# Differential attention weights: two diagonal products on TensorE per block, or one combination on VectorE and a transpose

## What is computed

```
s = jnp.einsum('bqhcd,bkhcd->bchqk', qi, kf) * scale
s = jnp.where(mask, s, NEG_INF)
p = jax.nn.softmax(s, axis=-1)
w = p[:, 0] - lam * p[:, 1]
return jnp.einsum('bhqk,bkhd->bqhd', w, vf)
```

## Time and profile before, and how to read it

| | |
|---|---|
| median of 3 runs | 3783.66 us (3781.82 to 3785.66) |
| the profiled execution | 3782.0 us |
| its span | 3780.2 us |
| PE, PEld, DVE, ACT, POOL busy | 3536.2, 3345.4, 2086.2, 1083.3, 1947.7 us |
| mean granted TensorE clock | 0.97 |
| stage_m in the span | about 469 to 869 us |

### The profile page before, as it was taken

The page is one execution under the profiler, slowest core; times in us unless marked ns, Lnnn a source line. Parts: engine busy times, 40 slices in busy tenths (PEclk is TensorE's granted clock), DMA queues, the critical chain, the costliest instruction groups (busy, mean ns, idle before and its releaser), DMA issues. The chain is left out here.

```text
span 3780.2 us, 57577 instructions
## 1 busy us (share of the span) xinstructions
PE 3536.2 (94%) x22880; PEld 3345.4 (88%) x22880; DVE 2086.2 (55%) x3740; ACT 1083.3 (29%) x1181; POOL 1947.7 (52%) x735
## 2 busy tenths in 40 slices
PE   8999967888897999999999999997999999999997
PEld 8988743547897999999999999997999999999997
DVE  4212076426102899975444544453677777777773
ACT  3111032334212232333333333332222222222222
POOL 3333207004334445665655666654676676666762
PEclk9999978898998999999999999998999999999999
DMA  5577676562321224777777777777778878777872
GB/s 215 199 289 297 235 181 222 173 216 103 140 107 71 85 91 163 261 284 277 277 277 285 280 276 276 286 270 284 285 282 305 296 282 301 295 286 293 301 290 95
DMA packets 254404, 891.46 MB, mean 236 GB/s; under 512 B 99057, under 2 KB 132338, under 8 KB 177266
## 3 DMA queue, kind: packets, MB, share of 16 engines
q1 hardware_dynamic: 179026, 548.32, 41.3%
q0 software_dynamic: 36864, 268.45, 17.3%
q10 hardware_dynamic: 38368, 72.83, 5.5%
HBM read 818.45 MB, written 68.71 MB: 235 GB/s over the span
## 5 line engine op out<-in xcount | busy, mean ns | idle before, releaser
L111 POOL TENSOR_TENSOR wl<-raw,wh 128x2048 fp32r<-128x2048 f32 x324 | 1524.5, 4705 | 1353.5 <-ACT wh L107 1353.4
L107 ACT ACTIVATE wh<-raw 128x2048 fp32r<-128x2048 f32 x324 | 620.4, 1915 | 2069.8 <-PE acc L1296 718.8
L1631 PE MATMUL acc<-vh,wh 128*128 128x392 f32 x2048 | 703.8, 344 | 43.7 <-DVEq L1682 21.9
L1294 PE MATMUL acc<-hh,wh 128*128 128x392 f32 x2048 | 709.7, 347 | 5.8 <-POOL wl L111 5.8
L1295 PE MATMUL acc<-hl,wh 128*128 128x392 f32 x2048 | 698.3, 341 | 0.0
L1632 PE MATMUL acc<-vl,wh 128*128 128x392 f32 x2048 | 696.3, 340 | 0.0
L1296 PE MATMUL acc<-hh,wl 128*128 128x392 f32 x2048 | 696.0, 340 | 0.0
L1633 PE MATMUL acc<-vh,wl 128*128 128x392 f32 x2048 | 695.4, 340 | 0.0
L126 PE MATMUL acc<-hh,wh 128*128 128x264 f32 x1984 | 566.8, 286 | 18.2 <-POOL hl L978 17.4
L127 PE MATMUL acc<-hl,wh 128*128 128x264 f32 x1984 | 561.2, 283 | 0.0
L128 PE MATMUL acc<-hh,wl 128*128 128x264 f32 x1984 | 559.7, 282 | 0.0
(11 more groups left out here) (316 smaller groups left out, 3904.0 us busy)
## 6 DMA issues: line engine op xcount, KB each, us to landing
raw<-units SPq DMA_DIRECT2D x324, 1024.0 KB
kr<-cache_k SPq DMA_DIRECT2D x128, 512.0 KB, 6.0
vr<-cache_v SPq DMA_DIRECT2D x128, 512.0 KB, 5.4
expert_acts<-ast ACTq DMA_DIRECT2D x128, 196.0 KB
expert_gates<-gs ACTq DMA_DIRECT2D x14, 1792.0 KB, 6.3
a<-expert_acts SPq DMA_DIRECT2D x32, 784.0 KB
g<-expert_gates SPq DMA_DIRECT2D x32, 784.0 KB
xt<-x_t SPq DMA_DIRECT2D x4, 1040.0 KB, 12.1
```

Of the source, the lines that this page charges most:

```text
L107: act.activation(m.wh[s][:, :, :], m.raw[s][:, :, :], ACT.Copy).then_inc(m.hi_done, 1)
L111: pool.tensor_tensor(m.wl[s][:, :, :], m.raw[s][:, :, :], m.wh[s][:, :, :].bitcast(F32), ALU.subtract).then_inc(m.lo_done, 1)
L1294: pe.matmul(o, m.wh[s][:, k, :], m.hh[:, k, NA:T], start=(k == 0), stop=False)
L1631: pe.matmul(o, m.wh[s][:, 4 * e + d, :], vh[gg][:, e, :], start=(e == 0), stop=False)
```

## The change

The two maps are combined before PE sees them. DVE multiplies the whole second map of a tile, in place, by minus lambda over its row sum, waits for that, and adds the first map times the reciprocal of its row sum, in place. PE turns each block of 128 keys with the identity, one transpose for each block. `dg` and DVE's wait for `weighed` go. Everything else, ACT's copies and the semaphores' counts too, is as before.

```diff
-    qkv = at("qkv", [P, 2, 3, NT]); ex = at("ex", [P, 2, 2, NT]); vtok = at("vtok", [P, 2, 4, P]); wT = at("wT", [P, 2, 4, P]); dg = at("dg", [P, 2, 2, P])
+    qkv = at("qkv", [P, 2, 3, NT]); ex = at("ex", [P, 2, 2, NT]); vtok = at("vtok", [P, 2, 4, P]); wT = at("wT", [P, 2, 4, P])
...
                     for kb in range(q + 1):
-                        for c in range(2):
-                            mm = pe.matmul(m.aux[:, 0, 128 * kb:128 * kb + 128], ex[:, q % 2, c, 128 * kb:128 * kb + 128], dg[:, q % 2, c, :],
-                                           start=(c == 0), stop=(c == 1))
+                        mm = pe.transpose(m.aux[:, 0, 128 * kb:128 * kb + 128], ex[:, q % 2, 0, 128 * kb:128 * kb + 128], m.ident[:, :])
                     mm.then_inc(S["weighed"], 1)
...
                     dve.wait_ge(S["exps"], 2 * it + 2)
-                    if it >= 2:
-                        dve.wait_ge(S["weighed"], it - 1)
                     for c in range(2):
                         x = dve.reciprocal(part(c, 3), part(c, 2))
                         if c == 1:
                             ch(x)
                             ch(dve.tensor_tensor(part(1, 3), part(1, 3), lam[:, 4:5], ALU.mult))
-                    for c in range(2):
-                        x = dve.tensor_scalar(dg[:, q % 2, c, :], m.ident[:, :], part(c, 3), None, ALU.mult)
-                    x.then_inc(S["scaled"], 1)
+                    one, two = (ex[:, q % 2, c, 0:128 * (q + 1)] for c in range(2))
+                    ch(dve.tensor_scalar(two, two, part(1, 3), None, ALU.mult))
+                    dve.scalar_tensor_tensor(one, one, part(0, 3), two, ALU.mult, ALU.add).then_inc(S["scaled"], 1)
```

## The result

The kernel with the change takes 3790.28 us (median of 20 runs, 3785.51 to 3798.12) against 3783.24 for the kernel before (20 runs, 3778.54 to 3790.16). The ratio is 1.0019, with an interval of 1.0013 to 1.0025: 7.0 us slower. The change forecast was 3.7 us the other way.

A forecast was written before the change was run, and what follows sets the result against it. No single engine bounds the stage, so each head was walked: -2.56 (heads 2, 5, 6, 7), -1.01, +1.92, -1.96 and -0.13 (heads 0, 1, 3, 4) sum to -3.7 us, giving 3780.0 us, range 3769 to 3792.

The forecast's parts named there:

- What bounds the stage: Stage from 469 to 869 us: PE is fullest, no single engine sets the pace, and nothing outside changes.
- rival (a): Whole stage: PE is the bound after all, so all 29.6 us come off, giving 3754; 12%.
- The prices: One q=3 tile: PE's 2.05 us becomes 0.63; DVE's 0.48 us pair becomes 0.480 plus 0.746.
- rival (d): PE's transposes run in two passes: q=3 saves 0.95 instead of 1.42, sum near -1, 3783; 4%.
- Heads 0, 1 and 3: Forecast -1.01, +1.92 and -1.96 us; in head 1 DVE is the path throughout and PE's savings count nothing.
- rival (c): Head 1: the two new DVE instructions collide with POOL, +6 over the sum, 3786; 6%.
- Head 4: DVE's +0.38 and +0.58 less 0.45 of slack, then -0.64: -0.13 us.
- Heads 2, 5, 6 and 7: Each saves 0.64 us, together -2.56.
- -0.64: Per head, at q=3: DVE's chain gets 0.78 us longer, then PE's tile 1.42 shorter.
- rival (b): PE's clock falls more often as its step 4 wait grows: +7.9 us, 3791.6; 15%.
- its wait doubles, 0.80 to 1.58: PE's wait in step 4 of a head, before q=3's tile, was said to grow from 0.80 to 1.58 us.
- its 0.76: PE's saving on the q=1 tile, in us; taken as worth nothing in head 5.

The follow-up runs named there:

- PE's part: The changed kernel with DVE making the two diagonal matrices again and PE transposing the first map alone, unscaled: 3778.22 us, ratio 0.9987 to the kernel before.
- filler: The changed kernel with eight useless f32 products on PE before the step 4 wait for DVE's weights, in heads 2, 4, 5, 6, 7: 3783.80 us, ratio 1.0001.
- DVE's part: The changed kernel with each block turned by two plain identity products instead of one transpose, DVE's new work kept: 3792.69 us, ratio 1.0029 to the kernel before.

## Why the prediction was wrong, point by point

**What bounds the stage: right.** Only the stage moved, and no single engine sets its pace. The page waits did not give way: 34.8 us against 32.6. That and the time refute rival (a): 31 us less of PE's work did not make the kernel shorter.

**The prices: right.** DVE's pair at q=3 is 0.49 and 0.75 (forecast 0.480 and 0.746), the tile follows its scores by 6.54 in heads 6 and 7 (6.5), four transposes take 0.66 (0.63), and the 80 records are busy for 19.1 (16 to 20), which also settles rival (d). These hold wherever the clock is as it was.

**Heads 0, 1 and 3: right,** within 0.5 us each in this pair of executions, which for heads 0 and 3 is closer than one pair can show, as said above. Head 1 is right in spite of POOL. Beside POOL the pairs there took 1.60, 2.47 and 1.93 us for q=1 to 3, well over the undisturbed 0.83, 1.04 and 1.24, so the direction of rival (c) is there; but the head grew by 1.88, as forecast, since dg had been stretched as well.

**Head 4: right by luck.** I had put it with the heads that escaped the clock. The kernel before has a fall of its own at that head's end, behind a wait of 4.49 us, where each product of L726 takes 0.42 us; in the kernel after the clock falls earlier and is back there, each takes 0.27:

```profile
752.93 0.37 PE L726 MATMUL aux<-qq,bb 64*16 64x128 f32 x1 [4.49 <-ACT km L527]
...
756.11 0.42 PE L726 MATMUL acc<-qq,bb 64*16 64x128 f32 x1
```

```profile
753.22 0.27 PE L724 MATMUL aux<-qq,bb 64*16 64x128 f32 x1 [0.83 <-ACT km L527]
```

The fall was moved, not added: from the first of these to the next scores it is 3.53 us before and 1.86 after.

**Heads 2, 5, 6 and 7: wrong, and with them the sign.** The step that failed is the sum "-0.64" for the plain heads. It says that what q=2 saves "only lengthens that wait", and costs the longer wait at nothing. That wait is what PE's clock answered to. The mechanism stood in rival (b), with its price (3791.6; the result is 3790.3), but at 15%, and the argument against it rested on a slip: "its wait doubles, 0.80 to 1.58". By my own terms the wait is 0.80, and 0.78 from DVE, and 1.10 from q=2's shorter tile: 2.68. Measured 2.63 and 2.65 in heads 6 and 7. Head 2 had lost the clock at 1.49; a wait of 1.58 could be told from that with some hope, one of 2.68 could not. With the right number (b) should have had the largest chance. What (b) said against itself, that head 6 ran at 1.00 and so had room, was no argument: a clock that is full with a wait of 0.80 says nothing of one three times as long.

That (b)'s price came so near is partly luck. It put the clock at 11.6 us, 2.9 for each plain head. The runs put it at 6 to 7: PE's part brought 6.3 less than its terms, and filler gave 6.8 back. The rest of the miss is the 3.3, not certain, that DVE's part cost above its terms.

The same step failed once more in head 5, for q=1. I put its 0.76 there at nothing, since PE waits for ACT behind it. It came out as 0.72, and that wait grew by as much, 1.49 to 2.20; ACT's part ends 6.37 us after the scores of q=2 in both kernels. The scores of q=3 behind the wait ran at the lower clock, 1.80 instead of 1.13. The kernel before, the kernel after, and the kernel with products as filler in five heads:

```profile
786.18 0.47 PE L754 MATMUL aux<-ident,ys 72*128 72x72 f32 x4 [1.49 <-ACT yg L621]
786.58 1.13 PE L642 MATMUL acc<-qkv 64*128 64x512 f32 x4
```

```profile
786.04 0.47 PE L752 MATMUL aux<-ident,ys 72*128 72x72 f32 x4 [2.20 <-ACT yg L621]
786.44 1.80 PE L642 MATMUL acc<-qkv 64*128 64x512 f32 x4
```

```profile
785.39 0.47 PE L756 MATMUL aux<-ident,ys 72*128 72x72 f32 x4 [2.21 <-ACT yg L621]
785.79 1.13 PE L642 MATMUL acc<-qkv 64*128 64x512 f32 x4
```

The third had the same work and the same wait there and kept its clock. So a single execution does not say at which wait the clock falls; that it falls more often with PE's lighter load is what all runs together say.

**What would show it wrong** was well chosen: "if the granted clock between 740 and 869 us falls below 0.9 (then (b))"; it is 0.86.

## What to carry to other kernels

Where PE waits for a chain on other engines, taking work from PE beside that chain only lengthens its idle time, and the idle time can cost its clock for the work behind it, which is on the path. So write down for each such wait how long it will be after the change, every saved term included, and what PE still does around it, and compare both with the waits in the same kernel at which the clock held and those at which it fell. Take that as odds and not as a limit: here the clock once fell and once held behind the same wait of 2.2 us. And if the wait can't be shortened, move real work into it: here that brought more than the change itself was expected to.

## What the runs showed of the hardware that I had not expected

- Put into a wait of PE, transposes held TensorE's clock as products did: granted clock 0.92 in the same window, ratios of 0.9995 with transposes and 1.0001 with products.
- Useless work made a kernel faster: 40 extra products (80 records, about 2 us a head in five heads) took 1.0019 to 1.0001.
- Beside POOL, DVE's multiplication by a number per partition of 256 to 512 elements went from 0.35 to 0.49 us up to 0.78 to 1.51, and the two-input one from 0.48 to 0.75 up to 0.82 to 1.09, in head 1. Of the pair at 128 elements the first went from 0.29 to 0.65 and the second from 0.35 to 1.38. For q=2 and 3:

```profile
579.43 1.51 DVE L885 TENSOR_SCALAR ex<-ex,stt 128x384 f32<-128x384 f32 x1
580.97 0.96 DVE L886 SCALAR_TENSOR_TENSOR ex<-ex,stt 128x384 f32<-128x384 f32 x1
...
591.40 0.84 DVE L885 TENSOR_SCALAR ex<-ex,stt 128x512 f32<-128x512 f32 x1
592.27 1.09 DVE L886 SCALAR_TENSOR_TENSOR ex<-ex,stt 128x512 f32<-128x512 f32 x1
```

The first of the four is stretched more than the wider one behind it, so its length there does not follow from its size alone. That it depends on what POOL does at that moment is likely and not shown.
